# Sparse attention with heads in pairs on row and column parts of the array

## What is computed

```python
pc = softmax(where(mc, q @ kc.T * scale, NEG_2))            # compressed blocks
o_c = pc @ vc
ps = softmax(where(causal & selected, q @ ks.T * scale, NEG_2))
o_s = ps @ vs                                               # branch "s"
pw = softmax(where(causal & in_window, q @ kw.T * scale, NEG_2))
o_w = pw @ vw                                               # branch "w"
out = g[..., 0:1] * o_c + g[..., 1:2] * o_s + g[..., 2:3] * o_w
mixed = concatenate([out * silu(z_nsa), y_lru * silu(z_lru), y_conv * silu(z_conv)])
x = x + mixed @ w_out
```

## Time and profile before

| | us |
|---|---|
| median of 3 runs | 2950.22 |
| profiled execution | 2948.79 |
| its span, first to last instruction | 2947.0 |
| PE busy | 2793.0 (95%) |
| DVE busy | 1504.0 (51%) |
| ACT busy | 1149.8 (39%) |
| GpSimd (POOL) busy | 1059.3 (36%) |

### The profile page before, as it was taken

The page is one execution under the profiler, slowest core; times in us unless marked ns, Lnnn a source line. Parts: engine busy times, 40 slices in busy tenths (PEclk is TensorE's granted clock), DMA queues, the critical chain, the costliest instruction groups (busy, mean ns, idle before and its releaser), DMA issues. The chain is left out here.

```text
span 2947.0 us, 37005 instructions
## 1 busy us (share of the span) xinstructions
PE 2793.0 (95%) x12850; PEld 2185.3 (74%) x12860; DVE 1504.0 (51%) x2736; ACT 1149.8 (39%) x1915; POOL 1059.3 (36%) x430
## 2 busy tenths in 40 slices
PE   7999999999999899898999999998999898999898
PEld 6857776678888688576666788885887776887676
DVE  2067544572323310875364633325788565788564
ACT  2234434252323333344342432324247443247443
POOL 4422112334444334121123444442347411347411
PEclk9999999999999999999999999999999999999999
DMA  4211111222232223111112322321223101224101
GB/s 157 92 58 51 43 36 44 86 79 93 94 106 86 86 79 99 36 53 41 36 53 76 100 95 90 104 95 57 86 93 129 44 29 51 86 93 133 40 32 49
DMA packets 60888, 220.28 MB, mean 75 GB/s; under 512 B 6880, under 2 KB 7008, under 8 KB 60640
## 3 DMA queue, kind: packets, MB, share of 16 engines
q1 hardware_dynamic: 60192, 217.12, 22.1%
q10 hardware_dynamic: 576, 1.57, 0.2%
HBM read 216.57 MB, written 2.10 MB: 74 GB/s over the span
## 5 line engine op out<-in xcount | busy, mean ns | idle before, releaser
L428 POOL TENSOR_TENSOR w_lo<-w_raw,w_hi 128x1024 fp32r<-128x1024 f32 x404 | 1009.2, 2508 | 1855.4 <-ACT w_hi L411 1842.5
L402 PE MATMUL bank<-x_hi,w_hi 128*128 128x512 f32 x2128 | 895.1, 421 | 47.4 <-DVE x_lo L2323 17.0
L404 PE MATMUL bank<-x_hi,w_lo 128*128 128x512 f32 x2128 | 838.2, 394 | 0.0
L403 PE MATMUL bank<-x_lo,w_hi 128*128 128x512 f32 x2128 | 837.4, 394 | 0.0
L411 ACT ACTIVATE w_hi<-w_raw 128x1024 fp32r<-128x1024 f32 x400 | 418.6, 1053 | 469.4 <-PE bank L404 457.9
L402 PEld LDWEIGHTS bank<-x_hi,w_hi 128*128 128x128 f32 x2128 | 406.0, 191 | 166.3 <-issue 56.2
L404 PEld LDWEIGHTS bank<-x_hi,w_lo 128*128 128x128 f32 x2128 | 404.3, 190 | 87.7
L403 PEld LDWEIGHTS bank<-x_lo,w_hi 128*128 128x128 f32 x2128 | 406.5, 191 | 83.1 <-issue 12.7
L402 PE MATMUL bank<-rhs_hi,w_hi 128*128 128x512 f32 (+1 forms) x656 | 262.3, 400 | 4.0 <-DVE rhs_lo L1427 4.0
L403 PE MATMUL bank<-rhs_lo,w_hi 128*128 128x512 f32 (+1 forms) x656 | 255.6, 390 | 0.0
L404 PE MATMUL bank<-rhs_hi,w_lo 128*128 128x512 f32 (+1 forms) x656 | 255.3, 389 | 0.0
(11 more groups left out here) (405 smaller groups left out, 3629.0 us busy)
## 6 DMA issues: line engine op xcount, KB each, us to landing
w_raw<-w SPq DMA_DIRECT2D x404, 512.0 KB, 3.4
ln_in<-x SPq DMA_DIRECT2D x1, 2048.0 KB, 7.9
out<-residual SPq DMA_DIRECT2D x8, 256.0 KB, 2.2
p_raw<-p ACTq DMA_DIRECT2D x2, 512.0 KB, 3.9
constants<-con SPq DMA_DIRECT2D x1, 455.0 KB, 3.3
cos<-cos SPq DMA_DIRECT2D x1, 256.0 KB, 3.5
sin<-sin SPq DMA_DIRECT2D x1, 256.0 KB, 3.7
params_b<-prm_b ACTq DMA_DIRECT2D x1, 256.0 KB, 2.6
```

Of the source, the lines that this page charges most:

```text
L402: nc.tensor.matmul(out, wh, xh, start=first, stop=False)
L403: nc.tensor.matmul(out, wh, xl, start=False, stop=False)
L404: S.last = nc.tensor.matmul(out, wl, xh, start=False, stop=last)
L428: S.nc.gpsimd.tensor_tensor(S.wl[s][:, :], S.raw[s][:, :], S.wh[s][:, :].bitcast(F32), ALU.subtract).then_inc(S.lo_ready[s], 1)
```

## The change

- Heads go in pairs, one of each key group: 32 pairs per layer (`HeadPair`), order head t, block b, branch s then w.
- Scores: no staged queries. Both heads' matmuls contract over 64 rows each, rows 0 to 63 and 64 to 127 of `S.q` and of the keys, into `S.X[0]` and `S.X[1]`. The two causal matmuls stay. These banks are single: scores of pair n + 1 wait for both exponentials of pair n.
- DVE: two row maxima, then per head reciprocal, gate, and a new pass that scales the probabilities in place in SBUF; the turning waits for it (`nsa_scaled`).
- ACT: both exponentials of pair n + 1, then the copies of both turned tiles of pair n (all 64 per layer; DVE copies none).
- Values: stationary 128 keys x 64 value columns, moving 128 queries, output to partitions 0 to 63 for one head and 64 to 127 for the other, feature-major, accumulated over both branches and the compressed term in PSUM. The compressed product becomes one more term of branch s (`S.cpt`, `S.vbd`).
- So the matmuls L1837, the copies L2267 and L1986, the stagings L1992 and L2214, the sums L1626 and the transposes L1848 go. Gate product and high/low parts (`mix`, `mix_hi`, `mix_lo`) of head pair k are done while pair k + 1 runs.
- `out_fill` keeps its 64 tiles, two per pair; columns of z and rows of the output projection are reordered on the host.

```diff
-    S.mnh, S.mnl = at("nsa_hi", [P, 4 * SEQ], F32R, 96), at("nsa_lo", [P, 4 * SEQ], F32R, 104)
+    S.mnh, S.mnl = at("nsa_hi", [P, 4 * SEQ], F32R, 142), at("nsa_lo", [P, 4 * SEQ], F32R, 118)
...
-    S.ot2 = at("b_o_tok", [P, QB * 512], F32, 142)
+    S.cpt = at("cmp_turned", [P, 2 * SEQ], F32, 150.5)
...
-def nsa_steps(S, L, i):
...
+class HeadPair:
+    def __init__(self, S, n):
+        t, r = divmod(n, 2 * QB)
+        self.t, (self.b, self.branch) = t, divmod(r, 2)
+        self.w = (self.b + 1) * P
+        self.key, self.value = ((S.kv["ks"], S.vtok["s"]), (S.kv["kw"], S.vtok["w"]))[self.branch]
+        self.bank = (S.ps[3], S.X[3])[t % 2]
+        self.probs, self.turned = ((S.wk[4:6], S.wk[6:8]), (S.wk[0:2], S.wk[2:4]))[n % 2]
+NPAIR = 4 * QB * 2
+def nsa_pe(S, pe, L, ident, fill):
+    nc = S.nc
+    Z, p0 = S.nsa, L * NPAIR
+    half = lambda e: slice(64 * e, 64 * e + 64)
+    def scores(n):
+        h = HeadPair(S, n)
+        if n >= 1:
+            pe.wait_ge(Z.p, 2 * (p0 + n))
+        for e in range(2):
+            nc.tensor.matmul(S.X[e][:, 0:h.w], S.q[half(e), h.t * SEQ + h.b * P:h.t * SEQ + h.w], h.key[half(e), 0:h.w],
+                             start=True, stop=False, skip_group_check=True)
+        for e in range(2):
+            nc.tensor.matmul(S.X[e][:, h.b * P:h.w], S.idb[:, :], S.causb[:, :], start=False, stop=True,
+                             skip_group_check=True).then_inc(Z.s, 1)
+    def turn(n):
+        h = HeadPair(S, n)
+        if n == 0:
+            pe.wait_ge(S.mc_y, L * 4 + 4)
+        for c in Z.ptc:
+            pe.wait_ge(c, p0 + n)
+        for e in range(2):
+            pe.wait_ge(S.nsa_scaled, 2 * (p0 + n) + e + 1)
+            for k in range(h.b + 1):
+                m = nc.tensor.transpose((S.X[2], S.ps[2])[e][:, k * P:(k + 1) * P], h.probs[e][:, k * P:(k + 1) * P], ident)
+            m.then_inc(Z.pt, 1)
+    def values(n):
+        h = HeadPair(S, n)
+        if n % (2 * QB) == 0 and h.t >= 2:
+            pe.wait_ge(S.mn_y, L * 4 + h.t - 1)
+        for c in Z.ptc:
+            pe.wait_ge(c, p0 + n + 1)
+        terms = []
+        if h.branch == 0:
+            c0 = lambda e: (2 * h.b + e) * P
+            terms.append(lambda e: (S.vbd[:, (4 * e + h.t) * HD:(4 * e + h.t + 1) * HD], S.cpt[:, c0(e):c0(e) + P]))
+        for k in range(h.b + 1):
+            terms.append(lambda e, k=k: (h.value[:, k * P + e * HD:k * P + (e + 1) * HD], h.turned[e][:, k * P:(k + 1) * P]))
+        for x, term in enumerate(terms):
             for e in range(2):
-                for b in range(QB):
-                    w = (b + 1) * P
-                    qk = [(S.wk[2 * tt + e][:, b * P:w], k[:, 0:w], 0, w),
-                          (S.idb[:, :], S.causb[:, :], b * P, P)]
-                    def v(kt, src=src, e=e):
-                        return S.vtok[src][:, kt * P + e * HD:kt * P + (e + 1) * HD]
-                    def scale(n, b=b, e=e, br=br, tt=tt):
-                        gate = cols2(S.gate, b * 3 * B_HEADS + e * 12 + tt * 3 + br, i, 6, 1)
-                        S.nc.vector.tensor_scalar(S.rg[n % 2][:, :], S.rinv[n % 2][:, :], gate, None, ALU.mult)
-                    def norm(n, b=b, e=e, tt=tt):
-                        o = cols2(S.ot2, b * 512 + e * 256 + tt * HD, i, 2 * HD, HD)
-                        S.nc.vector.scalar_tensor_tensor(out=o, in0=out_of(S, n), scalar=S.rg[n % 2][:, :], in1=o,
-                                                         op0=ALU.mult, op1=ALU.add).then_inc(S.nsa.out, 1)
-                    steps.append(Step(b, qk, v, norm, scale, () if b or e or br == 2 else staged))
-    if i == 0:
-        steps[2].ready += ((S.mc_y, L * 4 + 4),)
-    return steps
+class HeadPair:
+    def __init__(self, S, n):
+        t, r = divmod(n, 2 * QB)
+        self.t, (self.b, self.branch) = t, divmod(r, 2)
+        self.w = (self.b + 1) * P
+        self.key, self.value = ((S.kv["ks"], S.vtok["s"]), (S.kv["kw"], S.vtok["w"]))[self.branch]
+        self.bank = (S.ps[3], S.X[3])[t % 2]
+        self.probs, self.turned = ((S.wk[4:6], S.wk[6:8]), (S.wk[0:2], S.wk[2:4]))[n % 2]
+NPAIR = 4 * QB * 2
+def nsa_pe(S, pe, L, ident, fill):
+    nc = S.nc
+    Z, p0 = S.nsa, L * NPAIR
+    half = lambda e: slice(64 * e, 64 * e + 64)
+    def scores(n):
+        h = HeadPair(S, n)
+        if n >= 1:
+            pe.wait_ge(Z.p, 2 * (p0 + n))
+        for e in range(2):
+            nc.tensor.matmul(S.X[e][:, 0:h.w], S.q[half(e), h.t * SEQ + h.b * P:h.t * SEQ + h.w], h.key[half(e), 0:h.w],
+                             start=True, stop=False, skip_group_check=True)
+        for e in range(2):
+            nc.tensor.matmul(S.X[e][:, h.b * P:h.w], S.idb[:, :], S.causb[:, :], start=False, stop=True,
+                             skip_group_check=True).then_inc(Z.s, 1)
+    def turn(n):
+        h = HeadPair(S, n)
+        if n == 0:
+            pe.wait_ge(S.mc_y, L * 4 + 4)
+        for c in Z.ptc:
+            pe.wait_ge(c, p0 + n)
+        for e in range(2):
+            pe.wait_ge(S.nsa_scaled, 2 * (p0 + n) + e + 1)
+            for k in range(h.b + 1):
+                m = nc.tensor.transpose((S.X[2], S.ps[2])[e][:, k * P:(k + 1) * P], h.probs[e][:, k * P:(k + 1) * P], ident)
+            m.then_inc(Z.pt, 1)
+    def values(n):
+        h = HeadPair(S, n)
+        if n % (2 * QB) == 0 and h.t >= 2:
+            pe.wait_ge(S.mn_y, L * 4 + h.t - 1)
+        for c in Z.ptc:
+            pe.wait_ge(c, p0 + n + 1)
+        terms = []
+        if h.branch == 0:
+            c0 = lambda e: (2 * h.b + e) * P
+            terms.append(lambda e: (S.vbd[:, (4 * e + h.t) * HD:(4 * e + h.t + 1) * HD], S.cpt[:, c0(e):c0(e) + P]))
+        for k in range(h.b + 1):
+            terms.append(lambda e, k=k: (h.value[:, k * P + e * HD:k * P + (e + 1) * HD], h.turned[e][:, k * P:(k + 1) * P]))
+        for x, term in enumerate(terms):
             for e in range(2):
-                for b in range(QB):
-                    w = (b + 1) * P
-                    qk = [(S.wk[2 * tt + e][:, b * P:w], k[:, 0:w], 0, w),
-                          (S.idb[:, :], S.causb[:, :], b * P, P)]
-                    def v(kt, src=src, e=e):
-                        return S.vtok[src][:, kt * P + e * HD:kt * P + (e + 1) * HD]
-                    def scale(n, b=b, e=e, br=br, tt=tt):
-                        gate = cols2(S.gate, b * 3 * B_HEADS + e * 12 + tt * 3 + br, i, 6, 1)
-                        S.nc.vector.tensor_scalar(S.rg[n % 2][:, :], S.rinv[n % 2][:, :], gate, None, ALU.mult)
-                    def norm(n, b=b, e=e, tt=tt):
-                        o = cols2(S.ot2, b * 512 + e * 256 + tt * HD, i, 2 * HD, HD)
-                        S.nc.vector.scalar_tensor_tensor(out=o, in0=out_of(S, n), scalar=S.rg[n % 2][:, :], in1=o,
-                                                         op0=ALU.mult, op1=ALU.add).then_inc(S.nsa.out, 1)
-                    steps.append(Step(b, qk, v, norm, scale, () if b or e or br == 2 else staged))
-    if i == 0:
-        steps[2].ready += ((S.mc_y, L * 4 + 4),)
-    return steps
+                v, p = term(e)
+                m = nc.tensor.matmul(h.bank[half(e), h.b * P:h.w], v, p, start=(h.branch == 0 and x == 0),
+                                     stop=(h.branch == 1 and x == len(terms) - 1), skip_group_check=True)
+        m.then_inc(Z.o, 1)
+    scores(0)
+    for n in range(NPAIR):
+        if n + 1 < NPAIR:
+            scores(n + 1)
+        fill(2 * n)
+        turn(n)
+        fill(2 * n + 1)
+        values(n)
+def nsa_act(S, act, L, after):
+    nc = S.nc
+    Z, p0 = S.nsa, L * NPAIR
+    def exps(n):
+        h = HeadPair(S, n)
+        for e in range(2):
+            act.wait_ge(Z.max, 2 * (p0 + n) + e + 1)
+            if n >= 2:
+                act.wait_ge(Z.pt, 2 * (p0 + n - 2) + e + 1)
+            x = 2 * (n % 2) + e
+            nc.scalar.activation(h.probs[e][:, 0:h.w], S.X[e][:, 0:h.w], ACT.Exp, bias=S.nm[x][:, :],
+                                 accum_out=S.rs[x][:, :]).then_inc(Z.p, 1)
+    def copy(n):
+        h = HeadPair(S, n)
+        for e in range(2):
+            act.wait_ge(Z.pt, 2 * (p0 + n) + e + 1)
+            if n >= 2:
+                act.wait_ge(Z.o, p0 + n - 1)
+            nc.scalar.activation(h.turned[e][:, 0:h.w], (S.X[2], S.ps[2])[e][:, 0:h.w], ACT.Copy).then_inc(Z.ptc[e], 1)
+    exps(0)
+    for n in range(NPAIR):
+        if n + 1 < NPAIR:
+            exps(n + 1)
+        copy(n)
+        after(n)
+def nsa_dve(S, dve, L, after):
+    nc = S.nc
+    Z, p0 = S.nsa, L * NPAIR
+    def rowmax(n):
+        h = HeadPair(S, n)
+        for e in range(2):
+            dve.wait_ge(Z.s, 2 * (p0 + n) + e + 1)
+            nc.vector.tensor_reduce(S.nm[2 * (n % 2) + e][:, :], S.X[e][:, 0:h.w], AX, ALU.max, negate=True).then_inc(Z.max, 1)
+    def share(n, e):
+        h = HeadPair(S, n)
+        dve.wait_ge(Z.p, 2 * (p0 + n) + e + 1)
+        nc.vector.reciprocal(S.rg[e][:, :], S.rs[2 * (n % 2) + e][:, :])
```

(108 more changed lines are left out.)

14 lines of the change are left out of this document (3 added, 11 removed).

## The result

| | before | after |
|---|---|---|
| device time, median | 2948.62 us (2945.92 to 2951.44) | 2931.74 us (2931.22 to 2937.42) |
| span of the profiled execution | 2947.0 us | 2929.4 us |
| ratio | | 0.9946, 95% interval 0.9934 to 0.9959 |
| stage, layer 1: first products of L1837 (2307.40, before) or first scores (2307.56, after) to first product of the last projection | 156.4 us | 147.8 us |
| stage, layer 2, between the same products | 156.6 us | 148.5 us |

What follows compares the result with a forecast made beforehand. The chain through ACT was taken to bound the kernel: eight rounds of 17.5 us plus start, first-pair, clock and end terms gave 151.1 per layer against 156.4, -10.6 over two layers, so 2939 us, range 2915 to 2975.

Steps and rivals of the forecast that it cites:

- Columns side by side: Value products: the two heads' column halves overlap, 0.213 us per term for both heads, 2.56 per round.
- Rival 1: Value products of the two heads run one after the other: +41 us, 2979, or 2969 without the column switch; chance 20%.
- The chain of a round: Four head pairs, eight times a layer: scores, maximum, exponentials, copies, values in sequence through ACT, 17.5 us.
- the switch: PE changing between full array and row or column halves: 0.20 us each, three per pair, 2.4 per round.
- PE's own sum: All PE work in a round of four pairs, switches included: 15.9 us against 17.1 before, hidden under ACT's chain.
- Start: Stage start: ACT's two splits, four x_hi, table load and first two exponentials take 6.3 us per layer.
- the scalings beside GpSimd: First pair of a stage: its two scalings wait for two GpSimd passes, making it 3.0 us late.
- Half clock: First two pairs of a stage: granted clock 0.50 doubles PE's share of the chain, 2.5 us, bounds 0 and 5.
- End: Stage end: three quarters' high and low parts lie ready, nine matmuls cover the fourth, 0.2 us.
- Mid-stage scalings at 0: Ten GpSimd passes per layer that mid-stage scalings may meet fall into about 2.5 us of slack, costing 0.
- Rivals 2 and 3: 2: PE still the bound, 2913, chance 12%. 3: clock falls in mid-stage, +27 us, 2966, chance 8%.
- last pair: End of the rounds: the last pair has no successor's scores, -0.9 us per layer.

## Why the prediction was right, and where it was off

The direction and the mechanism held: the scores' chain through ACT became the bound, rounds stayed level, and the gain is at the edges. The size was short by 6.3 us, just over 3 per layer.

- **Columns side by side.** Taken 0.213 per term, measured 0.22. Rival 1 fell, and the reordered products showed that lost overlap is paid in full: +17 even when the halves still overlap in part.
- **The chain of a round: 17.5, measured 17.2, so 2.5 us of each layer.** Over sixteen steady pairs the links per round are: scores with masks until the maximum 4.45 (4.73 taken), maximum to exponential 2.10 (2.15), exponentials 4.20 (4.1), copies until the values 3.62 (3.3), values 2.85 (3.2). Two terms were too large and two too small. The step that failed in the scores is the switch: entering the row halves takes 0.09 behind the values' last pass, not 0.20. For the values I counted a weight load at the entry of each pair, 0.6 per round, which mostly lies within the time from the copies. The copies themselves are as taken (3.05 in four widths, 3.1 taken), but from the end of the second to the first value product it is 0.14 each, not 0.05.
- **PE's own sum, 15.9 with three switches.** With four it measured 15.9; with three PE is busy 97.09 of 110 us, about 15.2 of a round. Here the error is the price of the switches again; the total is right to 5% only. It had no effect while the chain was the bound, but it hid from me that turning the order round would bring 16 us and not 8.
- **Start, 6.3.** The second pair's scores start 6.1 behind the first's, so the queue of ACT was counted rightly. So were the scalings beside GpSimd: 3.0 forecast, 2.6 and 3.6 by the first round with and without scaling.
- **Half clock, 2.5.** The granted clock is 0.50 in 2314 to 2318 and 0.57 in the next 4 us, then 1.00. Without scaling the first round is still 1.9 us over the steady value, which is mostly this, so it came about 0.6 cheaper.
- **End.** The first product of the last projection follows the last value products at once, as forecast. But the nine products that should cover the last quarter were 0.8 short:

```profile
2455.37 0.50 PE L398 MATMUL bank<-nsa_hi,w_hi 128*128 128x512 f32 x1
2455.38 2.41 POOL L424 TENSOR_TENSOR w_lo<-w_raw,w_hi 128x1024 fp32r<-128x1024 f32 x1 [12.56 <-ACT w_hi L407]
...
2456.08 0.68 DVE L1767 TENSOR_TENSOR residual<-residual,bank 128x512 f32<-128x512 f32 x1
...
2456.86 1.47 DVE L2343 TENSOR_TENSOR nsa_lo<-silu_z_nsa,nsa_hi 128x512 fp32r<-128x512 f32 x1
...
2457.35 0.39 PE L400 MATMUL bank<-nsa_hi,w_lo 128*128 128x512 f32 x1
...
2458.39 0.50 PE L398 MATMUL bank<-nsa_hi,w_hi 128*128 128x512 f32 x1 [0.66 <-DVE nsa_lo L2343]
```

  `mix_lo(3)` (L2343) ended with GpSimd's subtraction. I had priced this edge at 0.2 and missed that meeting. Against it stands what I also left out: before, the clock fell behind the wait at the end in layer 2, which cost 1.6 us, and not in layer 1. That the two nearly cancel (the last projection lasts 26.2 us in both layers after, 25.2 and 26.8 before) is luck, as the forecast had neither.
- **Mid-stage scalings at 0.** Exactly so, 34.39 with them, 34.36 without. But the slack of 2.5 us was no protection, the timing was: in the version with the copy on DVE the same passes met GpSimd seven times a layer.
- **Rivals 2 and 3.** PE is busy 88%, not the bound; the clock is 1.00 in mid-stage although PE idles 0.5 us per pair on average, and up to 1.0 in one. Both fell for this kernel; the clock did fall in mid-stage of the version with the copy on DVE, behind waits of 1.81.

Adding up layer 1: 151.1, less 2.4 in the rounds, less 0.9 in first pair and clock, less 0.2 at the start, plus 0.2 at the last pair, is the measured 147.8; in layer 2 first pair and clock took 0.8 more, 148.5. With the last projection (+1.0 and -0.6) the sum over both layers is -16.3, the times say -16.9.

## What to carry to other kernels

When an engine at 99% gets less work, write out the closed chain of the new order before counting the gain: here about 2 us per round (12.9 of 110 us) of PE's time became waits, and only moving one step of the order (scores two pairs ahead) turned it into time. Test a link by lengthening it: if the period grows by the same amount, it is on the chain, whatever the busy shares say. A small pass that shares something with another engine should be priced by when it starts, not by its length; moving an unrelated copy can make it meet, or miss, the other's passes.
